# Layer norm of a convolution branch: centring behind a weight half's low part, and the variance part one weight half later

## What is computed

```python
u = glu_val * jax.nn.sigmoid(glu_gate)
u = causal_depthwise_conv(u, conv_b_w[l]) + conv_b_b[l]      # width 31
u = jax.nn.silu(layer_norm(u, ln_b_g[l], ln_b_b[l]))
y_b = u @ w_out_b[l] + b_out_b[l]
...
merged = gates[..., 0, :] * y_a + gates[..., 1, :] * y_b + gates[..., 2, :] * y_x
x = x + merged @ w_o[l]

def layer_norm(x, g, b):
    mu = jnp.mean(xf, axis=-1, keepdims=True)
    xc = xf - mu
    var = jnp.mean(xc * xc, axis=-1, keepdims=True)
    y = xc * lax.rsqrt(var + EPS) * g + b
```

## Time and profile before

| | |
|---|---|
| median of 3 executions | 880.46 us (880.23 to 880.76) |
| the profiled execution: its time | 880.85 us |
| its span | 879.1 us |
| busy in the span | PE 850.6, DVE 788.4, ACT 646.8, POOL 21.9 us |
| mean granted TensorE clock | 0.993 |

### The profile page before, as it was taken

One profiled execution on the slowest core, in us unless ns is written; L12 is line 12 of the kernel. 1 busy time (PEld: TensorE's weight loads), 2 busy tenths in 40 slices (PEclk: granted clock), 3 DMA queues, 4 the chain that ended last, 5 costly groups with the idle time before them and its releaser, 6 DMA issues.

```text
span 879.1 us, 14484 instructions
## 1 busy us (share of the span) xinstructions
PE 850.6 (97%) x5711; PEld 754.4 (86%) x5711; DVE 788.4 (90%) x776; ACT 646.8 (74%) x611; POOL 21.9 (2%) x30
## 2 busy tenths in 40 slices
PE   5999999999999999989999999999999999999996
PEld 5999999999889999867778888888888888888874
DVE  5448999999877776779999999999999999999996
ACT  6564424344553465476999999999999999999996
POOL 0110000000000000034000000000000000000000
PEclk9999999999999999989999999999999999999998
DMA  9943555444452359644999999999999999999961
GB/s 376 418 169 121 191 182 201 171 164 182 156 192 96 124 210 385 250 158 189 368 419 428 428 426 429 429 429 429 429 429 428 427 429 428 429 428 429 427 269 48
DMA packets 20151, 270.70 MB, mean 308 GB/s; under 512 B 2192, under 2 KB 2448, under 8 KB 3856
## 3 DMA queue, kind: packets, MB, share of 16 engines
q1 hardware_dynamic: 19552, 268.06, 74.8%
q10 hardware_dynamic: 560, 2.10, 0.7%
HBM read 269.10 MB, written 1.05 MB: 307 GB/s over the span
## 4 chain that ended last, share of the span: by engine, by line
PE 83%; DVE 12%; issue 2%; ACT 1%; DMA 1%; SPq 0%; DVEq 0%; ACTq 0%
PE ps L1464 24%; PE ps L1478 12%; PE ps L1283 9%; PE ps L1285 9%; PE ps L1284 9%; PE ps L1451 4%; PE ps L1488 3%; DVE lo L1048 3%; DVE lo L799 2%; DVE conv L886 2%; PE ps L1298 2%; PE ps L1300 2%; PE ps L1299 2%; PE ps L1563 2%; PE ps L1570 1%
## 5 line engine op out<-in xcount | busy, mean ns | idle before, releaser
L1048 DVE TENSOR_TENSOR lo<-raw,hi 128x2048 fp32r<-128x2048 f32 x142 | 319.2, 2284 | 1.2 <-ACT hi L636 1.2
L636 ACT ACTIVATE hi<-raw 128x2048 fp32r<-128x2048 f32 x141 | 264.8, 1914 | 20.0 <-PE ps L1464 19.9
L799 DVE TENSOR_TENSOR lo<-raw,hi 128x2048 fp32r<-128x2048 f32 x62 | 142.6, 2302 | 27.0 <-ACT hi L436 25.6
L1283 PE MATMUL ps<-inA,hi 128*128 128x256 f32 x576 | 164.3, 285 | 1.6 <-DVE lo L799 1.1
L436 ACT ACTIVATE hi<-raw 128x2048 fp32r<-128x2048 f32 x63 | 120.6, 1915 | 59.9 <-PE ps L1285 41.0
L1285 PE MATMUL ps<-inA,lo 128*128 128x256 f32 x576 | 163.0, 283 | 0.0
L1284 PE MATMUL ps<-inA,hi 128*128 128x256 f32 x576 | 163.0, 283 | 0.0
L1464 PE MATMUL ps<-hi,xeT 128*128 128x512 f32 x384 | 154.4, 402 | 1.3 <-issue 0.8
L1464 PE MATMUL ps<-lo,xeT 128*128 128x512 f32 x384 | 150.1, 391 | 0.0
L1283 PEld LDWEIGHTS ps<-inA,hi 128*128 128x128 f32 x576 | 110.5, 192 | 2.6 <-DVE lo L799 2.5
L1284 PEld LDWEIGHTS ps<-inA,hi 128*128 128x128 f32 x576 | 110.5, 192 | 0.1
(11 more groups left out here) (246 smaller groups left out, 1254.6 us busy)
## 6 DMA issues: line engine op xcount, KB each, us to landing
raw<-in_w_experts SPq DMA_DIRECT2D x96, 2048.0 KB, 11.7
raw<-in_w_dense SPq DMA_DIRECT2D x29, 2048.0 KB, 7.8
raw<-in_w_dense SPq DMA_DIRECT2D x2, 1024.0 KB, 8.1
x_sb<-in_x SPq DMA_DIRECT2D x1, 1024.0 KB, 4.9
mem_sb<-in_mem SPq DMA_DIRECT2D x1, 1024.0 KB, 15.5
x_again<-in_x ACTq DMA_DIRECT2D x1, 1024.0 KB, 5.0
ffn_row<-in_rows ACTq DMA_DIRECT2D x1, 512.0 KB, 7.6
raw<-in_rows SPq DMA_DIRECT2D x1, 512.0 KB, 3.6
```

The source lines that it names most:

```text
L636: nc.scalar.activation(expert_half(hi, N0), raw_flat(slot, k % 2), ACT.Copy).then_inc(hi_made, 1)
L799: nc.vector.tensor_tensor(conv_half(lo, N), raw_half(slot, h), conv_half(hi, N).bitcast(f32), ALU.subtract).then_inc(lo_made, 1)
L1048: nc.vector.tensor_tensor(expert_half(lo, N0), raw_flat(expert_slot(m), k % 2), expert_half(hi, N0).bitcast(f32), ALU.subtract).then_inc(l ...
L1283: mm(dst, w_hi[:, k, c * P:(c + 1) * P], acts[:, 0, k, :], start=(k == 0), stop=False)
```

## The change

Nothing is computed otherwise; five steps change their place.

- `ln_centre` (DVE, n=45) goes from ahead of lo(47) to behind it.
- `ln_variance` (DVE) goes from n=47, ahead of lo(49), to n=48, behind lo(50). `ln_scale` goes from behind lo(49) to behind `ln_variance`, still ahead of lo(51).
- `channel_sum(7)` (PE) goes from behind c(47) to behind c(48). `square_sum`, the reduce on DVE, stays where it was.
- `branch_b_act` (ACT) goes from n=47, behind hi(50), to n=48, behind the Sigmoid of c(48) and hi(51).
- `branch_b_hi` (ACT) goes from n=48, behind hi(51), to n=49, behind hi(52), and with it the issue of the DMA of `x_again`. `branch_b_lo` (DVE) goes from n=49, behind lo(51), to n=50, behind lo(52).

PE still waits for `b_lo` ahead of c(52).

```diff
@@ ACT's extras
-                     F["out_x"] + 1: [ln_squares], F["out_x"] + 3: [branch_b_act], F["gate1"]: [branch_b_hi],
+                     F["out_x"] + 1: [ln_squares], F["gate1"]: [branch_b_act], F["gate1"] + 1: [branch_b_hi],
@@ DVE's extras
-                     F["gate2"] + 3: [conv_sum], F["out_x"] + 2: [square_sum],
-                     F["out_x"] + 3: [ln_scale], F["gate1"] + 1: [branch_b_lo]}
-
-            urgent = {F["out_x"] + 1: ln_centre, F["out_x"] + 3: ln_variance}
+                     F["gate2"] + 3: [conv_sum], F["out_x"] + 1: [ln_centre],
+                     F["out_x"] + 2: [square_sum], F["gate1"]: [ln_variance, ln_scale], F["gate1"] + 2: [branch_b_lo]}
+
@@ DVE's loop
-                if n in urgent:
-                    urgent[n]()
@@ PE's extras
-                     F["out_x"] + 3: [lambda: channel_sum(7, ln_mean[:, :], squares_summed, ln_sumsq)],
+                     F["gate1"]: [lambda: channel_sum(7, ln_mean[:, :], squares_summed, ln_sumsq)],
```

## The result

The changed kernel takes 882.7 us (median of 12 executions, 881.1 to 883.2) against 880.8 us before (12, 880.15 to 881.74): a ratio of 1.0022, 95% interval 1.0014 to 1.003. It is 0.2% slower, where 880.9 us and no change were forecast, and it lies 0.1 us above the range. Beside later runs on another chip it was 882.64 against 880.71 us, 1.0014 (1.0005 to 1.0023).

The account below looks back on a forecast made before the run. PE, busy 97%, bounds the kernel, and its time follows c(52). Two waits removed (2.6 us) return as 0.4 at c(49) and 2.7 at c(52): 880.46 + 0.38, about 880.9 us; 8-in-10 range 880.0 to 882.6.

Parts of the forecast that it names:

- The two waits go: On PE, the layer norm's waits ahead of c(47) (0.9 us) and `channel_sum(7)` (1.4 us) disappear; 2.6 us with their starts.
- The small wait at c(49): On PE ahead of c(49), a new wait ended by lo(49), some 0.4 us.
- The chain to `b_lo`: From c(48)'s end over ACT and DVE to L929, ending at 335.83; c(52)'s second matmul at 336.10, against 335.72 before.
- Idle ahead of c(52): PE waits for `b_lo` from 333.3 on, some 2.6 us idle, before starting c(52) at 335.88.
- Table loads: On ACT, a table switch costs 1.3 us as in the rows, without the skill page's drain of 1.38; three loads as before.
- The rest costs nothing: hi(53), lo(53), the later DMA of `x_again`, SP's loads and GpSimd add no time.
- The time moves by as much as c(52) moves: w_o, router and experts hang on PE's results at c(52), so its shift is the whole time's shift.
- The clock falls in the new wait: Rival: PE's idle 2.6 us ahead of c(52) lowers its clock, losing 1.7 to 3.5 us; 882.6 to 884.4 us; chance 12%.
- the first rival: PE's clock falls in the new idle stretch ahead of c(52), making the kernel slower: 882.6 to 884.4 us; chance 12%.
- Its price: Cost of a clock fall at c(52): some 7 us at half speed lose 3.5 us, half that time 1.7 us.
- The start of the sum: The forecast adds 0.38 us to the earlier kernel's median of 880.46 us, 0.39 below its profiled execution.
- The hidden chain: Rival: `b_lo` is there by 333.1, c(52) starts at 333.16, a gain of 2.44 us: 878.0 us; chance 6%.

Follow-up runs that it names:

- the kernel with 20 fillers: Changed kernel plus 20 matmuls of 128x256, results never read, on PE between c(51) and the wait for `b_lo`; 881.07 us, ratio 1.0003 to the kernel before.
- where the chain was made to fit: Changed kernel with hi(52) between square root and Silus, a one-column Silu ahead of it, and `branch_b_hi` right behind `branch_b_act`; 878.58 us, ratio 0.9971.
- the experiment without the centring: Changed kernel with the centring put back ahead of lo(47), all else as changed; 883.36 us, ratio 1.003.
- the centring alone: Kernel before with only the change's first step, the centring moved behind lo(47); 881.6 us, ratio 1.0009.
- the kernel that waits for lo(53): Kernel before in which PE waits ahead of c(52) for lo(53), not lo(52); 882.57 us, ratio 1.0011.
- `rank_constants`: Kernel before in which PE also waits ahead of c(52) for ACT's `rank_constants`; 886.33 us, ratio 1.0058.

## Why the prediction was wrong

Point by point:

- **The two waits go**: right. Neither is in the list.
- **The small wait at c(49)**: 0.4 us forecast, 0.30 measured, ended by lo(49).
- **The chain to `b_lo`**: right to some hundredths. Forecast and measured less 0.48 us: the square root 319.51 and 319.46, the reciprocal 319.97 and 319.91, the first Silu 323.01 and 322.96, hi(52) 329.39 and 329.33, L929 333.55 and 333.48, the second matmul of c(52) 336.10 and 336.10.
- **Idle ahead of c(52)**: 2.6 us forecast, 2.4 in the list of waits. Sum +0.38 us: the kernel with 20 fillers, which has the whole change and no idleness, gave +0.34 (881.07 against 880.73).
- **Table loads**: the switches cost 1.3 us each as the rows said (318.65 to 319.94, 327.50 to 328.80). The drain that the Trainium skill (ScalarE: Activation LUTs, What ACT_TABLE_LOAD costs) adds does not show here either: hi(51) ends at 318.63 and the load starts at 318.65. By an estimate from that page's drain, two of them, c(52) would have come 2.8 us later.
- **The rest costs nothing**: right. `x_again` took 16.9 us instead of 5.0 and nobody waited for it.
- **The time moves by as much as c(52) moves**: right to within some 0.8 us in a single execution, by the router's part of it.
- **The clock falls in the new wait**: this is the step that failed. The forecast's sum put the clock at nothing, and gave its fall 12%; it fell for about 3.4 us at c(52), in both profiled executions of the changed kernel and, by the times, in 16 of 23. The mechanism, its place and its sign were those of the first rival. The argument against it was one gap of 1.44 us in one profiled execution, where the clock stayed at 1.00. That gap says nothing of one of 2.4 us, and one execution says nothing of a share. Counted by their times, the executions that seem to have lost the clock are none of 11 with 1.2 us idle, 2 of 11 with 1.8, 16 of 23 with 2.4, 8 of 11 with 2.9, about half of 11 with 2.6 us in another place, and probably 3 of 6 with 3.4. Some of them may be late for the other reason that the last section tells of.
- **Its price**: 1.7 to 3.5 us forecast, 1.5 measured. I took half speed as twice the time. At full clock a matmul of 256 columns starts every 0.12 us, at a granted 0.50 every 0.213: it becomes 1.78 times as long, not 2.
- **The start of the sum**: the forecast stands on 880.46, the median of three executions; twelve gave 880.8. So 880.46 + 0.38 + 1.5 = 882.3 would still have been in the range, and 880.8 + 0.38 + 1.5 = 882.7 is what was measured. That the result lies 0.1 us beyond the range and not inside is these 0.34 us; that it is slower at all is the clock.
- **The hidden chain**, 6%: it didn't come by this change, but its price was right. Forecast were 2.44 us; where the chain was made to fit, c(52) came 2.42 us earlier (333.30 against 335.72). The medians give 2.4 us (878.58 against 881.0); without the late executions of both kernels it is 2.2.

## What to carry to other kernels

When steps are moved so that a wait goes, look where the next consumer picks them up, and add up every row between: here two waits of 2.6 us together became one of 2.4 us plus 0.3, to within 0.4 us of the sum, and the slack of 3.75 us at c(52) was all spent. Idle time of TensorE isn't additive: in one piece of 2.4 us between full matmuls it cost the clock in most executions, in two pieces of 0.9 and 1.4 us or with 10 or 20 filler matmuls it didn't. If a stall can't be removed, fill it; if the activation engine switches tables inside such a chain, put the copies, which needed no table load of their own here, and the consumer's operand ahead of the switch back.

## What the runs showed of the hardware

**Whether the clock falls is a matter of the execution.** The same kernel with the same idle stretch keeps it or loses it: 7 and 16 of 23 at 2.4 us, by the times. It may fall some 0.4 us before PE starts again (335.4 against 335.80), about when it does (336.4 against 336.3) or well into dense matmuls (at about 338.5, 1.5 us behind the start at 336.98, in the experiment without the centring). A stretch of 3.4 us was seen without a fall, and so was one of 2.6 us (the centring alone). The low level lasted about 3.4 us in each of these three profiles. What decides it in a given execution stays open.

**The granted clock in the profile isn't always the one that PE runs at.** Some executions of several kernels, the one before among them (2 of 12 in the first measurement, 2 of 33, 9 of 20 and 5 of 28 in the later ones), lie 0.9 to 2.2 us above the median of the rest; in the later three their mean clock is 0.993 to 0.995, like that of the others. A profile of such an execution is that of the kernel that waits for lo(53); its first matmuls, at the start of the span:

```profile
14.58 0.41 PE L1284 MATMUL ps<-inA,hi 128*128 128x256 f32 x1
14.79 0.41 PE L1285 MATMUL ps<-inA,lo 128*128 128x256 f32 x1
15.01 0.42 PE L1283 MATMUL ps<-inA,hi 128*128 128x256 f32 x1
```

against the kernel before:

```profile
14.40 0.28 PE L1284 MATMUL ps<-inA,hi 128*128 128x256 f32 x1
14.52 0.28 PE L1285 MATMUL ps<-inA,lo 128*128 128x256 f32 x1
14.63 0.28 PE L1283 MATMUL ps<-inA,hi 128*128 128x256 f32 x1
```

They come 0.21 us apart, the pace of the lower level, while the window says 1.00:

```profile
14.00:16.00 2.00, 1.77 (x8) 1.80 (x9) 2.00 (x7) 2.00 (x3) 0.00 (x0) 1.00 0.94 401
```

and c(45) and c(51) end 1.5 us later than before. How many matmuls this slow start takes differs: 16 in this profile, 18 in that of `rank_constants` (1.62 us), about 5 in that of the changed kernel (0.48 us), none in that of the kernel before. That the late executions of the other kernels have the same cause is likely, from their size, but none of them was profiled. The distance between matmuls is the surer sign of the clock than the column.
